# Encoder layer with an expert-choice MoE: the final norm moved beside the last expert, and the order of the last prompt tile and of expert 0 changed

## Chip, cores and metric

One core of a Trainium2 chip. The time is device microseconds of one execution; the kernel is one launch. The engines are named as in the profile: PE (TensorE matmul), PEld (its weight loads), ACT (ScalarE), DVE (VectorE), POOL (GpSimd), SP (SyncE, which issues most DMAs).

## The reference

Two request groups, 256 prompt tokens and 1024 sample tokens with model width 1024, pass one encoder layer with the same weights: adaLN modulation, two attention branches, an output projection, then a mixture of experts in which each expert chooses its tokens, and a final RMSNorm.

```python
h2 = rms_norm(x, norm2_g) * (1 + sc2) + sh2
x = x + gt2 * expert_choice_moe(h2, w_router, w_e_gate, w_e_up, w_e_down)   # per group
y = rms_norm(x)                                                              # gain norm_f_g

def expert_choice_moe(h, ...):      # t: (n, d)
    aff = softmax(t @ w_router)     # 16 experts
    g, idx = top_k(aff.T, 2 * n // 16)        # 32 prompt rows, 128 sample rows per expert
    xe = t[idx]
    hid = silu(xe @ w_gate) * (xe @ w_up)     # width 2048
    out = zeros.at[idx].add((hid @ w_down) * g)
```

All arithmetic is float32. The kernel builds each float32 product from three bf16 products.

## The kernel before

**Precision.** Each matrix is split in a high bf16 half (a cast) and a low bf16 half (the value less the high half). `split_product` multiplies high by high, high by low and low by high (lines 1620 to 1622).

**Experts.** For an expert, `gate_up(f)` makes 128 of the 2048 hidden columns for 160 rows (128 sample, 32 prompt), f from 0 to 15. ScalarE takes the SiLU (L1142), VectorE multiplies by the up part (L1552, `product`), GpSimd splits the hidden values in halves (L816, L819). `down` multiplies by the down weights (L1621, and L1986 for the prompt rows). The down products of expert e run inside expert e+1; those of the last expert stand alone at the end. VectorE evacuates them in `evacuate_down` (L1531, L1533) with the router's weight and the gate.

**Weights.** An expert has 12 chunks of 2 MB, four each of gate, up and down. A chunk is loaded by SP into one of three float32 stages, by kind. ScalarE casts its two halves (L895), VectorE subtracts (L1515, `split_low`, which raises `lo_done`), and the bf16 halves stand in one of six slots. SP waits for `lo_done` of both halves before it loads the stage anew (L628, L634). Expert 0's first eight halves (0 to 7) are prepared beforehand, their low halves by GpSimd (`low_first`, L727). In expert 0 ScalarE does, for each f, the cast of half f+8 and then the SiLU of f, while VectorE does the subtraction of half f+8 and then product f. Halves 8 to 15 are the rest of expert 0 (8, 9 gate; 10, 11 up; 12, 13 gate; 14, 15 up); after them come halves of expert 1 and the down chunk of expert 0.

**The order of steps.** `plan_steps` writes a list that all engines walk. For a token tile `O` is the output product, `XO` the residual add and norm, `X2` the turn to columns with modulation, `RT` the router product and its exponential, `AT` the turn of the scores. `OL` is the output product of the last prompt tile in four parts (two for each column half), `XS` turns and modulates the gathered sample rows of expert 0, `FH` and `FL` are high and low halves of expert 0's first weights, `KM`/`K`/`IS`/`I` are the top-k and its indices. Engines wait for each other by semaphores alone.

**Gather and scatter.** An expert's rows are gathered from memory by an indirect DMA of GpSimd (L716), turned on TensorE, modulated on VectorE and split on GpSimd. Results are added to the accumulator in memory by two indirect DMAs (L828 sample, L830 prompt rows in quarters of 256 columns); L836 follows when they have landed. The prompt rows of expert 0 have their own path: turned at L1954, modulated at L1519, split on GpSimd at L850 and L853, behind `low_first(5)` and `low_first(6)`.

**End.** SP waits for the last expert's down products and its scatter, loads the gain and all ten tiles of 128 rows (L692, L694); ScalarE squares and sums (L1165), VectorE scales to a mean (L1580), ScalarE takes the root (L1167), VectorE the reciprocal (L1582) and the product (L1583), and SP stores (L697).

Of the kernel before, what the change touches and what calls it, by code (L numbers as in the profile page):

```python
# [19 lines left out]
ALU = mybir.AluOpType  # L20
# [80 lines left out]
def plan_steps(items):  # L101
# [98 lines left out]
    for m in range(KD):  # L200
# [5 lines left out]
        for _ in range((0, 0, 2, 3, 3, 3, 3, 2)[m]):  # L206
# [4 lines left out]
          ("FL", 3), ("OL", 0), ("OL", 1), ("X2", ns), ("OL", 2), ("RT", ns), ("OL", 3), ("AT", ns), ("XO", ns + 1),  # L211
          ("X2", ns + 1), ("XS",), ("RT", ns + 1), ("AT", ns + 1)]
# [19 lines left out]
def encoder(nc, x_p, x_s, c_p, c_s, w_ada, b_ada, n1g, w_in, qg, kg, sink, w_ba, w_bb, w_out, n2g, w_router,  # L232
# [25 lines left out]
    with ExitStack() as ctx:  # L258
# [91 lines left out]
        nfb = at(2 * NT * D, D)  # L350
        fin = at(0, NT, D)
        finy = at(10240, NT, D)
# [91 lines left out]
        f_ss, f_v, f_sq, y_ready, y_out = sem("f_ss"), sem("f_v"), sem("f_sq"), sem("y_ready"), sem("y_out")  # L444

# [104 lines left out]
        def _(sp):  # L550
# [138 lines left out]
            sp.wait_ge(dn_done, 8 * NE)  # L689
            sp.wait_ge(sca[0], 16 * NE)  # L690
            sp.wait_ge(sca[1], 16 * NE)
            sp.dma_start(nfb, nfg.partition_broadcast(P)).then_inc(nf_in, 16)  # L692
            for t in range(NT):
                sp.dma_start(fin[:, t], token_rows(acc_d, t)).then_inc(f_in[t], 16)  # L694
            for t in range(NT):
                sp.wait_ge(y_ready, t + 1)
                sp.dma_start(token_rows(y_d, t), finy[:, t]).then_inc(y_out, 16)  # L697
# [4 lines left out]
        def _(gp):  # L702
# [26 lines left out]
            for s in steps:  # L729
# [56 lines left out]
                if k == "XO" and s[1] == NT - 1:  # L786
# [7 lines left out]
                    gp.tensor_tensor(dst[:, 1], xs32, dst[:, 0], ALU.subtract)  # L794
# [44 lines left out]
            for b in range(2):  # L839
# [17 lines left out]
            def expert_pool(e, par, first=False, last=False):  # L857

                h0 = 11 * e + 4
# [21 lines left out]
            scatter(NE - 1, 4 * NE - 2)  # L881
# [3 lines left out]
        def _(ac):  # L885
# [277 lines left out]
            for t in range(NT):  # L1163
                ac.wait_ge(f_in[t], 16)
                ac.activation(finy[:, t], fin[:, t], ACT.Square, accum_out=rs[:, t % 2, 4:5]).then_inc(f_ss, 1)  # L1165
                ac.wait_ge(f_v, t + 1)
                ac.activation(rs[:, t % 2, 6:7], rs[:, t % 2, 5:6], ACT.Sqrt).then_inc(f_sq, 1)  # L1167


        @block.vector  # L1170
        def _(ve):
# [27 lines left out]
            def modulate(s, dst, A, sh, g, halves=(0, 1)):  # L1199

                for half in halves:
# [5 lines left out]
                    ins.then_inc(free, 1)  # L1207

# [42 lines left out]
            for s in steps:  # L1251
# [177 lines left out]
                if k == "M2":  # L1429
# [4 lines left out]
                    if b:  # L1434
                        ins.then_inc(mm_ready, 1)
                if k == "XO":
# [6 lines left out]
                    ve.wait_ge(xo_in[t % 2], 16 * (t // 2 + 1))  # L1443
                    if t >= 2:
                        ve.wait_ge(x1_out[t % 2], 16 * (t // 2))
                    if t < NT - 1:
# [4 lines left out]
                        norm_in(NT + t)  # L1451
                    else:
                        for h in range(2):
                            z = slice(512 * h, 512 * h + 512)
                            ve.wait_ge(*((half_done, 1), (out_done, NT))[h])
                            ve.tensor_tensor(x1[:, t % 2, z], ps[:, 2 * (t % 2) + h], gt1b[g][:, z], ALU.mult).then_inc(last_mul, 1)
                            ve.wait_ge(last_mul, h + 1)
                            ve.tensor_tensor(x1[:, t % 2, z], x1[:, t % 2, z], xo[:, t % 2, z], ALU.add).then_inc(x1_half, 1)
                        ve.wait_ge(ssq, 2 * NT + 1)
                        link(ve.tensor_tensor(rs[:, t % 2, 0:1], rs[:, t % 2, 0:1], rs[:, t % 2, 4:5], ALU.add))  # L1460
                        norm_in(NT + t)
# [54 lines left out]

            ve.wait_ge(xe_done, 3)
# [3 lines left out]
            ins.then_inc(xe_mod, 3)  # L1521

# [13 lines left out]
            def expert_vec(e, par, kind):  # L1536
# [518 lines left out]
```

## Time and profile before

| what | value |
|---|---|
| median of 3 runs (range) | 2432.73 us (2430.87 to 2434.41) |
| the profiled execution, its time | 2433.03 us |
| its span, first to last instruction | 2431.2 us |
| mean granted TensorE clock | 0.98 |
| PE busy | 2317.6 us, 95% |
| DVE busy | 1629.0 us, 67% |
| ACT busy | 1216.5 us, 50% |
| POOL busy | 1109.1 us, 46% |
| DMA moved | 523.29 MB, mean 215 GB/s |

Busy time is the time in which an engine had an instruction in work; the span leaves out what lies around it, so the profiled execution's own time is 1.8 us longer. Row times are microseconds from the span's start. The experts run from 1073 us to 2392 us.

### The profile page before, as it was taken

The numbers are of one execution on the slowest core, as the hardware profiler recorded it, in microseconds if no ns is written. First come the engines' busy times: TensorE is split into PE (matmuls) and PEld (weight loads), VectorE is DVE, ScalarE is ACT, GpSimd is POOL, SyncE is SP. The second block draws the span as 40 slices with busy tenths as digits, with TensorE's granted clock in tenths as the row PEclk, the third lists the DMA queues.
The fourth block names the chain that finished last, engine by engine and source line by source line (L and its number), as shares of the span: only waits on it lengthen the run. The fifth ranks groups of instructions, "written<-read, shape, count | busy, mean of one in ns | idle before, by whom it ended". The sixth has DMA issues, their size and how long they took to land.

```text
span 2431.2 us, 54392 instructions
## 1 busy us (share of the span) xinstructions
PE 2317.6 (95%) x23617; PEld 1688.2 (69%) x23724; DVE 1629.0 (67%) x2034; ACT 1216.5 (50%) x1536; POOL 1109.1 (46%) x706
## 2 busy tenths in 40 slices
PE   8998999999999999959999999999999999999993
PEld 3554676665444457748888888888888888888871
DVE  4765665464222455848887888788779887887872
ACT  4224555475111235345666555655565565556552
POOL 0000111122322214466566776677667766776641
PEclk9998999999999999979999999999999999999997
DMA  9102101502212345378999999989998999999965
GB/s 332 36 18 87 36 1 36 174 1 62 52 53 52 104 157 156 106 254 281 323 331 318 317 334 326 319 317 332 333 320 319 321 342 313 317 327 337 315 246 203
DMA packets 252293, 523.29 MB, mean 215 GB/s; under 512 B 8491, under 2 KB 57756, under 8 KB 251932
## 3 DMA queue, kind: packets, MB, share of 16 engines
q1 hardware_dynamic: 241500, 488.38, 57.6%
q0 software_dynamic: 10560, 31.46, 4.6%
q8 instruction: 188, 3.08, 0.5%
q14 instruction: 45, 0.37, 0.0%
HBM read 491.50 MB, written 28.31 MB: 214 GB/s over the span
## 4 chain that ended last, share of the span: by engine, by line
PE 88%; DVE 4%; DMA 3%; ACT 2%; issue 2%; POOL 1%; SPq 1%; DVEq 0%; ACTq 0%; POOLq 0%
PE ps L1621 23%; PE ps L1622 22%; PE ps L1620 22%; PE ps L1792 4%; PE ps L1780 4%; PE ps L1986 4%; PE ps L1761 3%; DMA arena<-w_e_up 1%; PE ps L1771 1%; PE ps L1681 1%; DMA arena<-w_in 1%; PE ps L1633 1%; PE ps L1719 1%; PE ps L1801 1%; PE ps L1945 1%
## 5 line engine op out<-in xcount | busy, mean ns | idle before, releaser
L1621 PE MATMUL ps<-arena 128*128 128x160 bf16 (+2 forms) x5554 | 1387.9, 268 | 9.7 <-issue 3.0
L1622 PE MATMUL ps<-arena 128*128 128x160 bf16 (+2 forms) x5556 | 1388.4, 268 | 0.3
L1620 PE MATMUL ps<-arena 128*128 128x160 bf16 (+2 forms) x5463 | 1354.3, 266 | 10.7 <-POOL arena L853 6.4
L1515 DVE TENSOR_TENSOR arena<-arena 128x2048 bf16<-128x2048 f32 x376 | 918.8, 2447 | 204.7 <-ACT arena L895 204.2
L895 ACT ACTIVATE arena<-arena 128x2048 bf16<-128x2048 f32 x384 | 726.8, 1904 | 249.1 <-PE ps L1622 179.7
L1620 PEld LDWEIGHTS ps<-arena 128*128 128x128 bf16 x5560 | 545.3, 98 | 166.5 <-issue 14.9
L1622 PEld LDWEIGHTS ps<-arena 128*128 128x128 bf16 x5560 | 545.4, 98 | 153.1 <-issue 0.8
L1621 PEld LDWEIGHTS ps<-arena 128*128 128x128 bf16 x5560 | 545.4, 98 | 140.8 <-issue 1.1
L819 POOL TENSOR_TENSOR arena<-arena 128x320 bf16<-128x320 f32 x128 | 273.8, 2139 | 10.0
L816 POOL TENSOR_TENSOR arena<-arena,ones 128x320 bf16<-128x320 f32 x128 | 176.2, 1376 | 173.0 <-DVE arena L1552 172.7
L1142 ACT ACTIVATE arena<-ps 128x160 f32<-128x160 f32 x256 | 77.5, 303 | 295.3 <-PE ps L1622 295.1
L738 POOL TENSOR_TENSOR arena<-ones,rinv 128x512 f32<-128x512 f32 x20 | 20.9, 1043 | 338.4 <-DVE rinv L1390 279.8
L1427 DVE TENSOR_TENSOR arena<-arena,ps 128x512 f32<-128x512 f32 x32 | 20.6, 684 | 177.9 <-ACT arena L1080 177.9
L1016 ACT ACTIVATE arena<-ps 128x512 f32<-128x512 f32 (+2 forms) x160 | 74.5, 494 | 100.3 <-PE ps L1780 95.7
L805 POOL TENSOR_TENSOR arena<-arena,ones 128x480 bf16<-128x480 f32 (+1 forms) x45 | 103.0, 2288 | 39.6 <-DVE arena L1507 39.5
L1780 PEld LDWEIGHTS ps<-ident,arena 128*128 128x128 f32 x752 | 82.1, 143 | 54.9 <-issue 43.6
L1080 ACT ACTIVATE arena<-ps 128x512 f32<-128x512 f32 x32 | 17.4, 595 | 203.1 <-PE ps L1622 203.1
L755 POOL TENSOR_TENSOR arena<-arena 128x512 f32<-128x512 f32 (+1 forms) x24 | 26.1, 1088 | 193.5 <-DVE arena L1427 171.4
L1780 PE MATMUL ps<-ident,arena 128*128 128x128 f32 x752 | 110.6, 285 | 3.1 <-ACT arena L1005 1.4
L1552 DVE TENSOR_TENSOR arena<-arena,ps 128x160 f32<-128x160 f32 x256 | 79.8, 312 | 41.7 <-POOL arena L819 41.5
L1792 PE MATMUL ps<-arena 128*64 128x128 f32 x1504 | 101.6, 281 | 5.9 <-ACT arena L1016 5.0
L1363 DVE TENSOR_REDUCE nm<-ps 128x1 f32<-128x1024 f32 (+1 forms) x80 | 81.2, 1059 | 38.4 <-PE ps L1761 32.1
(229 smaller groups left out, 2246.8 us busy)
## 6 DMA issues: line engine op xcount, KB each, us to landing
arena<-w_e_gate SPq DMA_DIRECT2D x64, 2048.0 KB, 9.1
arena<-w_e_up SPq DMA_DIRECT2D x64, 2048.0 KB, 9.5
arena<-w_e_down SPq DMA_DIRECT2D x64, 2048.0 KB, 9.0
arena<-w_ada SPq DMA_DIRECT2D x12, 2048.0 KB, 9.0
arena<-w_in SPq DMA_DIRECT2D x30, 512.0 KB, 5.3
arena<-x_sample SPq DMA_DIRECT2D x16, 512.0 KB, 3.6
arena<-w_in SPq DMA_DIRECT2D x3, 2048.0 KB, 16.6
arena<-w_out SPq DMA_DIRECT2D x2, 2048.0 KB, 9.1
```

Source lines behind the costliest of these rows:

```text
L805: gp.tensor_tensor(xeT[par][:, 0, d0:d1], src, ones[:, 0:d1 - d0].unsqueeze(2).to_broadcast([P, d1 - d0, SLOTS]), ALU.mult).then_inc(high, 1)
L816: gp.tensor_tensor(hidT[par][:, 0, f:f + 2], src, ones[:, 0:2].unsqueeze(2).to_broadcast([P, 2, SLOTS]), ALU.mult).then_inc(high, 1)
L819: gp.tensor_tensor(hidT[par][:, 1, f:f + 2], src, hidT[par][:, 0, f:f + 2], ALU.subtract).then_inc(hid_done, 1)
L895: ac.activation(split_half(slot, a)[0], stage_half(kind, a), ACT.Copy).then_inc(hi_done, 1)
L1363: ve.tensor_reduce(nm[:, i % 4, hh:hh + 1], src, AX.X, ALU.max, negate=True).then_inc(nm_ready, 1)
L1515: ve.tensor_tensor(lo, stage_half(kind, a), hi, ALU.subtract).then_inc(lo_done, 1)
L1620: pe.matmul(out, w_hi, x_hi, start=start, stop=False)
L1621: pe.matmul(out, w_hi, x_lo, start=False, stop=False)
L1622: return pe.matmul(out, w_lo, x_hi, start=False, stop=stop)
L1780: ins = pe.transpose(b[:, q * P:(q + 1) * P], probs(i, hh)[:, (a + q) * P:(a + q + 1) * P], ident[:])
L1792: ins = pe.matmul(ps[hh * 64:hh * 64 + 64, 4, j * P:(j + 1) * P], V[:, br, kt, hh * 64:hh * 64 + 64], PTs[br][:, i % 2, hh, n, :], start=( ...
L1986: ins = pe.matmul(ps[32 * g:32 * g + 32, banks[2], 0:256], x, wv[n][:, kf, 256 * g:256 * g + 256], start=q + kf == 0 and x is x_hi and n = ...
```

## The change

In words:

1. The final norm's loads wait for the scatter of expert 14, not of expert 15. The norm is written in place (`fin`), the squares go to a scratch area, and the mean of tile t+1 is computed before the reciprocal of tile t. The last expert's results are not scattered with an add: GpSimd gathers the accumulator's rows that they belong to, VectorE adds, ScalarE squares, a one-column matmul sums the four quarters of the prompt rows, and the finished rows are written over the output by two indirect DMAs after all plain stores have landed. VectorE takes up the last evacuation after six tiles of the norm.
2. The first column half of the last prompt tile (`XH`) goes ahead of the router step of the tile before; `XO` of the last tile does the second half alone and goes ahead of `AT` of the tile before. `XS` goes ahead of `X2` of the first prompt tile.
3. The prompt rows of expert 0 are split by VectorE; GpSimd's `low_first(6)` waits until this is done.
4. In expert 0 VectorE does product f and then the subtraction of half f+7 (`splits(f - 1)`).

```diff
-          ("FL", 3), ("OL", 0), ("OL", 1), ("X2", ns), ("OL", 2), ("RT", ns), ("OL", 3), ("AT", ns), ("XO", ns + 1),
-          ("X2", ns + 1), ("XS",), ("RT", ns + 1), ("AT", ns + 1)]
+          ("FL", 3), ("OL", 0), ("OL", 1), ("XS",), ("X2", ns), ("XH",), ("OL", 2), ("RT", ns), ("OL", 3), ("XO", ns + 1),
+          ("AT", ns), ("X2", ns + 1), ("RT", ns + 1), ("AT", ns + 1)]
...
-            sp.wait_ge(dn_done, 8 * NE)
-            sp.wait_ge(sca[0], 16 * NE)
-            sp.wait_ge(sca[1], 16 * NE)
+
+            sp.wait_ge(lo_done, 24 * NE)
+            sp.wait_ge(xe_done, 3 * NE)
             sp.dma_start(nfb, nfg.partition_broadcast(P)).then_inc(nf_in, 16)
+            for g in range(4):
+                sp.dma_start(nfP[32 * g:32 * g + 32], nfg[256 * g:256 * g + 256].partition_broadcast(32)).then_inc(nf_in, 16)
+            sp.wait_ge(sca[0], 16 * (NE - 1))
+            sp.wait_ge(sca[1], 16 * (NE - 1))
             for t in range(NT):
                 sp.dma_start(fin[:, t], token_rows(acc_d, t)).then_inc(f_in[t], 16)
             for t in range(NT):
                 sp.wait_ge(y_ready, t + 1)
...
             low_first(5)
+            gp.wait_ge(xe_ready, 3)
             low_first(6)
-            gp.wait_ge(xe_mod, 3)
-            dst = xeT[0][:, :, :, CAP_S:SLOTS]
-            gp.tensor_tensor(dst[:, 0], xp32, ones[:, 0:KD].unsqueeze(2).to_broadcast([P, KD, CAP_P]), ALU.mult)\
-                .then_inc(high, 2)
-            gp.wait_ge(high, 3)
-            gp.tensor_tensor(dst[:, 1], xp32, dst[:, 0], ALU.subtract).then_inc(xe_ready, 3)
             low_first(7)
...
-            scatter(NE - 1, 4 * NE - 2)
+
+            def by_quarter(x):
+                return x.rearrange("t (g n) -> (t g) n", g=4)
+
+            gp.tensor_copy(sidx[0][:], idx4[:, NE - 1:NE]).then_inc(cidx, 1)
+            gp.tensor_copy(sidx[1][:], idx[1][:, NE - 1:NE]).then_inc(cidx, 1)
+            gp.wait_ge(cidx, 4 * NE)
+            gp.wait_ge(xe_done, 3 * NE)
+            turn(1)
+            gp.indirect_dma_start(out=rowS, out_offset=None, in_=acc_d[1],
+                                  in_offset=bass.IndirectOffsetOnAxis(ap=sidx[1][:, 0:1], axis=0)).then_inc(gat[1], 16)
+            gp.indirect_dma_start(out=rowP, out_offset=None, in_=by_quarter(acc_d[0]),
+                                  in_offset=bass.IndirectOffsetOnAxis(ap=sidx[0][:, 0:1], axis=0)).then_inc(gat[0], 16)
+            gp.wait_ge(y_out, 16 * NT)
+            gp.wait_ge(row_ready[1], 1)
+            turn(0)
+            gp.indirect_dma_start(out=y_d[1], out_offset=bass.IndirectOffsetOnAxis(ap=sidx[1][:, 0:1], axis=0),
+                                  in_=yeS, in_offset=None).then_inc(row_out[1], 16)
+            gp.wait_ge(row_ready[0], 1)
+            gp.indirect_dma_start(out=by_quarter(y_d[0]), out_offset=bass.IndirectOffsetOnAxis(ap=sidx[0][:, 0:1], axis=0),
+                                  in_=yeP[:], in_offset=None).then_inc(row_out[0], 16)
+            for b in range(2):
+                gp.wait_ge(row_out[b], 16)
...
+            ac.wait_ge(lo_done, 24 * NE)
+            squares(0)
+            for t in range(1, NT):
+                squares(t)
+                root(t - 1)
+            for h in range(2):
+                ac.wait_ge(row_add, h + 1)
+                ac.activation(junk[:, 2, 512 * h:512 * h + 512], yeS[:, 512 * h:512 * h + 512], ACT.Square,
+                              accum_out=rs[:, h, 0:1]).then_inc(f_ss, 1)
+            ac.wait_ge(row_add, 3)
+            ac.activation(junk[:, 3, 0:256], yeP[:], ACT.Square, accum_out=rs[:, 1, 2:3]).then_inc(f_ss, 1)
+            root(NT - 1)
...
+            def last_half(h):
+
+                t = NT - 1
+                z = slice(512 * h, 512 * h + 512)
+                ve.wait_ge(*((half_done, 1), (out_done, NT))[h])
+                ve.tensor_tensor(x1[:, t % 2, z], ps[:, 2 * (t % 2) + h], gt1b[0][:, z], ALU.mult).then_inc(last_mul, 1)
+                ve.wait_ge(last_mul, h + 1)
+                ve.tensor_tensor(x1[:, t % 2, z], x1[:, t % 2, z], xo[:, t % 2, z], ALU.add).then_inc(x1_half, 1)
...
+            ve.wait_ge(out_done, NT)
             ve.wait_ge(xe_done, 3)
             for d in range(KD):
                 ins = ve.tensor_scalar(xp32[:, d], ps[:, 6, d * CAP_P:(d + 1) * CAP_P], A2[:, d, 0:1], modT[:, 24 + d, 0:1],
                                        ALU.mult, ALU.add)
             ins.then_inc(xe_mod, 3)
+            ve.wait_ge(xe_mod, 3)
+            dst = xeT[0][:, :, :, CAP_S:SLOTS]
+            link(ve.tensor_copy(dst[:, 0], xp32))
+            ve.tensor_tensor(dst[:, 1], xp32, dst[:, 0], ALU.subtract).then_inc(xe_ready, 3)
...
                 if kind == "first":
                     for f in range(KF):
-                        if f < KF - 1:
-                            splits(f)
                         product(f)
+                        if f:
+                            splits(f - 1)
                         if f in (7, 9, 11):
                             modulate_rows(3, (f - 7) // 2, 1)
                     splits(KF - 1)
...
+            mean(0)
+            ve.wait_ge(nf_in, 16 * 5)
+            for t in range(NT):
+                if t == 6:
+                    evacuate_down(NE - 1)
+                    ve.wait_ge(gat[1], 16 * NE + 16)
+                    for h in range(2):
+                        x = yeS[:, 512 * h:512 * h + 512]
+                        ve.wait_ge(ye_done, 3 * NE - 1 + h)
+                        ve.tensor_tensor(x, x, rowS[:, 512 * h:512 * h + 512], ALU.add).then_inc(row_add, 1)
+                    ve.wait_ge(gat[0], 16 * NE + 16)
+                    ve.wait_ge(ye_done, 3 * NE + 1)
+                    ve.tensor_tensor(yeP[:], yeP[:], rowP, ALU.add).then_inc(row_add, 1)
+                if t + 1 < NT:
+                    mean(t + 1)
                 ve.wait_ge(f_sq, t + 1)
                 link(ve.reciprocal(rs[:, t % 2, 7:8], rs[:, t % 2, 6:7]))
-                ve.scalar_tensor_tensor(out=finy[:, t], in0=fin[:, t], scalar=rs[:, t % 2, 7:8], in1=nfb,
+                ve.scalar_tensor_tensor(out=fin[:, t], in0=fin[:, t], scalar=rs[:, t % 2, 7:8], in1=nfb,
                                         op0=ALU.mult, op1=ALU.mult).then_inc(y_ready, 1)
+                if t == NT - 2:
+                    ve.wait_ge(f_ss, NT + 2)
+                    link(ve.tensor_tensor(rs[:, 0, 1:2], rs[:, 0, 0:1], rs[:, 1, 0:1], ALU.add))
+                    ve.tensor_scalar(rs[:, 0, 2:3], rs[:, 0, 1:2], 1.0 / D, EPS, ALU.mult, ALU.add).then_inc(f_v, 1)
+                    ve.wait_ge(row_sum, 1)
+                    ve.tensor_scalar(rst[:, 0, 1:2], ps[:, 0, 0:1], 1.0 / D, EPS, ALU.mult, ALU.add).then_inc(f_v, 1)
+            ve.wait_ge(f_sq, NT + 1)
+            link(ve.reciprocal(rs[:, 1, 1:2], rs[:, 0, 3:4]))
+            ve.scalar_tensor_tensor(out=yeS, in0=yeS, scalar=rs[:, 1, 1:2], in1=nfb, op0=ALU.mult, op1=ALU.mult)\
+                .then_inc(row_ready[1], 1)
+            ve.wait_ge(f_sq, NT + 2)
+            link(ve.reciprocal(rst[:, 0, 3:4], rst[:, 0, 2:3]))
+            ve.scalar_tensor_tensor(out=yeP[:], in0=yeP[:], scalar=rst[:, 0, 3:4], in1=nfP, op0=ALU.mult, op1=ALU.mult)\
+                .then_inc(row_ready[0], 1)
...
+            pe.wait_ge(fold_ready, 1)
+            pe.wait_ge(f_ss, NT + 3)
+            pe.wait_ge(prod_done, 16 * NE)
+            pe.matmul(ps[:, 0, 0:1], fold.rearrange("p a b -> p (a b)"), rs[:, 1, 2:3], start=True, stop=True).then_inc(row_sum, 1)
```

## Rows read from the trace of the kernel before

**Rows 1.** Windows, expert loop: us, PE to POOL busy (count), PEclk, DMA share, GB/s.
```profile
1160.00:1240.00 80.00, 79.69 (x1042) 66.37 (x1044) 65.35 (x59) 46.99 (x40) 41.10 (x24) 1.00 0.91 312
```

**Rows 2.** Timelines, last prompt tile, DVE and ACT: start us, us, instruction, [idle before].
```profile
1042.14 0.69 DVE L1456 TENSOR_TENSOR arena<-ps,arena 128x512 f32<-128x512 f32 x1
...
1049.49 2.90 ACT L1071 ACTIVATE arena<-ps,modT,A 128x128 f32<-128x128 f32 x8
...
1051.52 0.17 DVE L1469 TENSOR_REDUCE rst<-ps 128x1 f32<-128x16 f32 x1 [3.04 <-PE ps L1925]
```

**Rows 3.** Timelines, split of expert 0's prompt rows, DVE and POOL.
```profile
1066.99 1.84 DVE L1519 TENSOR_SCALAR arena<-ps,A,modT 128x32 f32<-128x32 f32 x8 [4.97 <-PE ps L1954]
...
1063.82 8.09 POOL L727 TENSOR_TENSOR arena<-arena 128x2048 bf16<-128x2048 f32 x2
1071.85 0.63 POOL L850 TENSOR_TENSOR arena<-arena,ones 128x256 bf16<-128x256 f32 x1
```

**Rows 4.** Timeline of SP's queue, loads of expert 0's weights.
```profile
1067.93 0.37 SPq L628 DMA_DIRECT2D arena<-w_e_gate  x1
1077.34 0.37 SPq L628 DMA_DIRECT2D arena<-w_e_up  x1
1083.78 0.37 SPq L628 DMA_DIRECT2D arena<-w_e_gate  x1
```

**Rows 5.** Timelines, expert 0, ACT (cast, SiLU) and DVE (product, subtraction).
```profile
1087.53 1.91 ACT L895 ACTIVATE arena<-arena 128x2048 bf16<-128x2048 f32 x1 [5.62 <-DMA arena<-w_e_up]
1089.35 0.29 ACT L1142 ACTIVATE arena<-ps 128x160 f32<-128x160 f32 x1
...
1091.68 0.31 DVE L1552 TENSOR_TENSOR arena<-arena,ps 128x160 f32<-128x160 f32 x1
1091.91 2.29 DVE L1515 TENSOR_TENSOR arena<-arena 128x2048 bf16<-128x2048 f32 x1
...
1120.50 3.15 DVE L1515 TENSOR_TENSOR arena<-arena 128x2048 bf16<-128x2048 f32 x1 [1.24 <-ACT arena L895]
```

**Rows 6.** Timeline of POOL, the last two scatters.
```profile
2377.30 0.19 POOL L836 TENSOR_TENSOR spare<-ones 128x1 f32<-128x1 f32 x1 [3.47 <-DMA acc_prompt<-yeP,sidx_p]
...
2393.85 0.19 POOL L798 TENSOR_TENSOR spare<-ones 128x1 f32<-128x1 f32 x1 [16.12 <-DVE yeP L1533]
...
2401.40 0.19 POOL L836 TENSOR_TENSOR spare<-ones 128x1 f32<-128x1 f32 x1 [3.49 <-DMA acc_prompt<-yeP,sidx_p]
```

**Rows 7.** Timeline of DVE, last evacuation and final norm.
```profile
2391.90 1.41 DVE L1531 SCALAR_TENSOR_TENSOR arena<-ps,gv_s,arena 128x512 f32<-128x512 f32 x2 [22.33 <-PE ps L1986]
...
2409.98 1.28 DVE L1583 SCALAR_TENSOR_TENSOR arena<-arena,rs 128x1024 f32<-128x1024 f32 x1
2411.18 0.15 DVE L1580 TENSOR_SCALAR rs<-rs 128x1 f32<-128x1 f32 x1
...
2426.33 1.28 DVE L1583 SCALAR_TENSOR_TENSOR arena<-arena,rs 128x1024 f32<-128x1024 f32 x1
```

**Rows 8.** Timeline of ACT, first tile of the final norm.
```profile
2407.09 1.06 ACT L1165 ACTIVATE arena<-arena 128x1024 f32<-128x1024 f32 x1 [41.55 <-DMA arena<-acc_prompt]
...
2408.25 1.28 ACT L1167 ACT_TABLE_LOAD   x1
```

**Rows 9.** The page's DMA issues: count, KB each, us to landing.
```profile
arena<-x_sample SPq DMA_DIRECT2D x16, 512.0 KB, 3.6
```

**Rows 10.** DMA issues 1020 to 1045: KB each, us from issue to landing.
```profile
arena<-w_e_gate SPq DMA_DIRECT2D x1, 2048.0 KB, 8.1
```

**Rows 11.** Expert 1's start (timelines), then PE by windows: us, busy, PEclk, DMA.
```profile
1136.09 0.32 DVE L1552 TENSOR_TENSOR arena<-arena,ps 128x160 f32<-128x160 f32 x1 [0.20 <-ACT arena L1142]
...
1136.55 0.23 PE L1620 MATMUL ps<-arena 128*128 128x160 bf16 x1 [0.84 <-DVE arena L1552]
...
1122.00:1124.00 2.00, 0.06 (x1) 1.00 1.05 402
1124.00:1126.00 2.00, 2.00 (x17) 0.52 0.50 179
```

More of the change, by code:

```diff
@@ L857, in expert_pool @@
             def expert_pool(e, par, first=False, last=False):
-                h0 = 11 * e + 4
+                h0 = 11 * e + 3
                 if not last:
@@ L1162, in _, with squares, root @@
             expert_act(NE - 1, "last")
-            for t in range(NT):
+            def squares(t):
                 ac.wait_ge(f_in[t], 16)
-                ac.activation(finy[:, t], fin[:, t], ACT.Square, accum_out=rs[:, t % 2, 4:5]).then_inc(f_ss, 1)
+                ac.activation(junk[:, t % 2], fin[:, t], ACT.Square, accum_out=rs[:, t % 2, 4:5]).then_inc(f_ss, 1)
+            def root(t):
                 ac.wait_ge(f_v, t + 1)
                 ac.activation(rs[:, t % 2, 6:7], rs[:, t % 2, 5:6], ACT.Sqrt).then_inc(f_sq, 1)
+            ac.wait_ge(lo_done, 24 * NE)
[10 more added lines that the diff above has]
+            root(NT - 1)
+            ac.wait_ge(f_v, NT + 1)
+            ac.activation(rs[:, 0, 3:4], rs[:, 0, 2:3], ACT.Sqrt).then_inc(f_sq, 1)
+            ac.wait_ge(f_v, NT + 2)
+            ac.activation(rst[:, 0, 2:3], rst[:, 0, 1:2], ACT.Sqrt).then_inc(f_sq, 1)
         @block.vector
@@ L1435, in _ @@
                         ins.then_inc(mm_ready, 1)
+                if k == "XH":
+                    ve.wait_ge(xo_in[(NT - 1) % 2], 16 * (NT // 2))
+                    ve.wait_ge(x1_out[(NT - 1) % 2], 16 * ((NT - 1) // 2))
+                    last_half(0)
                 if k == "XO":
@@ L1450, in _ @@
                         ve.tensor_tensor(x1[:, t % 2], x1[:, t % 2], xo[:, t % 2], ALU.add).then_inc(x1_ready, 1)
-                        norm_in(NT + t)
                     else:
[L1453 to L1458, printed above, removed]
+                        last_half(1)
                         ve.wait_ge(ssq, 2 * NT + 1)
                         link(ve.tensor_tensor(rs[:, t % 2, 0:1], rs[:, t % 2, 0:1], rs[:, t % 2, 4:5], ALU.add))
-                        norm_in(NT + t)
+                    norm_in(NT + t)
                     ve.tensor_scalar(xn2[:, t % 2], x1[:, t % 2], rs[:, t % 2, 3:4], None, ALU.mult).then_inc(xn2_ready, 1)
@@ L1575, in _ @@
             expert_vec(NE - 1, 1, "last")
-            evacuate_down(NE - 1)
-            ve.wait_ge(nf_in, 16)
-            for t in range(NT):
+            ve.wait_ge(xe_done, 3 * NE)
+            link(ve.tensor_tensor(fold[:, 0], ident[:, 0:32], ident[:, 32:64], ALU.add))
+            for g in (2, 3):
+                link(ve.tensor_tensor(fold[:, 0], fold[:, 0], ident[:, 32 * g:32 * g + 32], ALU.add))
+            ve.tensor_copy(fold[:, 1:4], fold[:, 0:1].to_broadcast([P, 3, 32])).then_inc(fold_ready, 1)
@@ L1579, in _, with mean @@
+            def mean(t):
                 ve.wait_ge(f_ss, t + 1)
                 ve.tensor_scalar(rs[:, t % 2, 5:6], rs[:, t % 2, 4:5], 1.0 / D, EPS, ALU.mult, ALU.add).then_inc(f_v, 1)
+            mean(0)
[13 more added lines that the diff above has]
+                    mean(t + 1)
@@ L1999, in expert_tensor @@
             def expert_tensor(e, par, kind):
+                if kind == "first":
+                    pe.wait_ge(high, 2)
                 pe.wait_ge(xe_ready, 3 * e + 3)
```

18 lines of the change are left out of this document (10 added, 8 removed).

## The prediction, made before the change was timed

> **What bounds the kernel now.** I read the windows view first: in an expert of the steady loop TensorE is busy 79.69 of 80 us at the full granted clock [rows 1]. Nothing in that loop is edited, and whatever moves the start of expert 1 moves the end by the same amount, because there is no idle TensorE time behind it to absorb a delay or to give back a gain. So the change can act in two places only: the passage from the last prompt tile to expert 1, and the tail behind the last down product. The chain of waits and the timelines by engine then show what is late in each.
>
> In the passage the order is: last prompt tile, router, top-k, gather, modulation, GpSimd's split of the prompt rows, first gate/up product [rows 2, 3]. From there TensorE is not the bound but the refill of the two weight stages: a 2 MB load, two ScalarE casts, two VectorE subtractions, and only then the next load into that stage [rows 4, 5]. In the tail TensorE has finished when the last evacuation starts at 2391.90, and the span ends at 2431.2: 39.3 us in which a scatter, a reload of all rows and ten tiles of norm run one behind the other [rows 6 to 8].
>
> **The tail, step by step.** SP no longer waits for the last expert's scatter but for the one before, which is over when GpSimd's L836 runs at 2377.30 [rows 6]. Issued at 2377.4, the first 512 KB tile lands after 3.6 us, the median of such loads [rows 9], at 2381.0. ScalarE squares two tiles (1.15 us each with the accumulator read, from 2407.09 to 2408.25), loads the Sqrt table (1.28) and takes the root (0.2) [rows 8]: 2384.8. Reciprocal and product take 0.2 and 1.28 [rows 7], so tile 0 is ready at 2386.3. Before, one tile took 1.81 us, because VectorE and ScalarE waited for each other; now the mean of the next tile is computed ahead and VectorE's own work is the bound: 1.20 from the product's start to the mean's start, 0.08 and 0.20 for the two small ones [rows 7], 1.5 us a tile. Tiles 0 to 5 are ready at 2393.8. That is 1.9 us after the last down product, so the evacuation now waits for VectorE and not for TensorE.
>
> Evacuation takes 1.8 us [rows 7]; three adds of the gathered rows, two of 512 elements at 0.61 to 0.69 [rows 2] and one of 256 at an estimated 0.4, 1.7 us: 2397.3. Tiles 6, 7, 8: 2401.8. One add and two means for the special rows, 0.5 us as ScalarE's squares and TensorE's 1-column product lie beside tiles 7 and 8; tile 9: 2403.9. Its store lands 3.6 us later, as before (product ends 2427.61, span ends 2431.2) [rows 7]: 2407.5. VectorE's two products on the special rows (1.7 us) lie inside that landing. GpSimd then turns over and issues two indirect stores; the same pair took from 2393.85 to 2401.40, 7.55 us, before [rows 6], where it added to memory. I take the same for the plain form, and 1.5 less as the other bound. End: 2415.1, against 2431.2, so **-16.1 us**. The new read of the last expert's rows by GpSimd starts at 2378 and is needed at 2395; the new broadcasts of the gain are issued at 2368. Both have 10 us of cover. The tile loads are issued in one stretch on SP and no store waits behind them before 2386. Bounds: -17.6 (faster store) and -12.5 (loads that land at the 5.3 us seen in the old reload, and 2 us of waiting between ScalarE and VectorE).
>
> **The passage, up to expert 0.** The first half of the last tile (two operations of 0.69) and the copy of the router's transposed scores leave VectorE's path ahead of the second half; the second half, which started at 1042.14 [rows 2], can start when TensorE's last output product of the tile ends, 1040.2: -1.9. ScalarE's eight modulations of the sample rows (2.90 from 1049.49) stood in front of the exponential, whose operand was ready at 1051.7 [rows 2]: -0.5. They go to a place where ScalarE idled six microseconds for the router, and TensorE's eight transposes go into its idle stretch 1030.3 to 1032.26, behind a gather that landed in 4.4 us at 1030.6. Top-k, indices and gather thus come 2.4 us earlier. Bounds: 1.0 (the gather lands late and holds TensorE's queue, behind it the tile's own transposes) and 2.4.
>
> The prompt rows' split: VectorE's modulation ended at 1068.83 [rows 3], now 1066.4. Two operations of 256 elements, 0.3 to 0.45 each from half the 0.69 row [rows 2], give 1067.2. GpSimd did it at 1071.85 to 1073.3, behind two low halves [rows 3]. So TensorE starts expert 0 6 us earlier. This is worth nothing by itself: the first SiLU stands on ScalarE behind the cast of a half whose load lands later. What counts is when loads start. GpSimd's low half 5 ends 2.4 us earlier, so the gate load goes at 1065.5 and not 1067.93. Low halves 6 and 7 now wait for 1067.2 and take 8.1 us [rows 3]: the up load goes at 1075.3 and not 1077.34 [rows 4], **-2.0**.
>
> **VectorE's order in expert 0.** Before, it did split(f), product(f). Now it does product(f), split(f-1). ScalarE's order is unchanged: cast(f), then SiLU(f). Halves 9 and 10 lie in different stages. The subtraction of half 9 frees the gate stage. Before, it ran ahead of product 1, and the next gate load was issued at 1083.78 while the up load of 1077.34 was in flight [rows 4]. Now it runs behind product 2, which needs SiLU 2, which stands behind the cast of half 10, the first of the **up** load. So each load is issued only after the other stage's load has landed: the overlap of two loads is gone.
>
> One link of this new chain: cast started to SiLU started 1.82 us; to the product 0.33; product start to subtraction start 0.23; subtraction 2.3 [rows 5]: 4.7 us, then a lone load. Lone loads of 2 MB took 8.1, three of them [rows 10]; add 0.1 to the cast. A link is 12.9 us, for one load. Before, two loads shared one turn of some 16.9: the up load of 1077.34 was cast from 1087.53 and its stage was free again at 1094.2 [rows 4, 5].
>
> The first up load took 10.19 to its cast at 1087.53 [rows 4, 5], with the next gate load and expert 1's rows beside it; now only the rows are beside it, and I take 9.5, between 8.2 and 10.2: cast at 1084.8. Five links follow (gate, up, gate, up of the next chunks, and the load that SiLU 14 waits for): 1084.8 + 64.5 = 1149.3. Product 14 at 1151.5, one subtraction, product 15 at 1154.0, first product of expert 1 0.46 later [rows 11]: 1154.5, where it was 1136.55. **+18.0 us** including the -2.0. TensorE idles some 3.5 us ahead of it. After 2 us of idling at 1122 to 1124 it came back at 0.52 of its clock for over 3 us [rows 11], which costs half of that: **+1.6**. Together +19.6. Bounds: 16.6 (no clock loss, first load 8.2) and 24 (rival B).
>
> A page speaks against the size of this term. The Trainium skill, "DMA: Bandwidth & Descriptors", section "Anatomy of one DMA", gives a load a fixed 2.0 us and 436 GB/s beyond that, thus an estimated 6.8 us for 2 MB; the front would then be 7 us less, and the time 2429.6. The trace disagrees (8.1 us), and the sum goes by the trace.
>
> **Sum.** 2431.2 + 19.6 - 16.1 = 2434.7. The profiled execution took 2433.03, 1.8 us more than its span: 2436.5. The median of the runs is 0.3 lower than that execution: 2436.2, in round numbers **2436.4**, +0.15%. A measurement of this kernel can tell about 0.2% (4.9 us) from no change, so the forecast is no change that can be told, leaning to slower. Its own range is 2430 to 2441.
>
> **Rivals.** A: the refill keeps its overlap (I misread which subtraction frees which stage, or the weight casts run ahead of the SiLU). Then the front gives its 2.0 us and the tail 16.1: 2414.6. For it speaks that TensorE starts earlier and that VectorE has idle time in this stretch; against it, that ScalarE's rows show cast, SiLU, cast, SiLU in strict turn [rows 5]. Chance 0.14.
>
> B: slower than forecast. The subtraction sits in each link, and beside GpSimd's splits it took 3.15 us and not 2.29 [rows 5]. The new order puts it right behind a product, which is what releases GpSimd. If all five links and the two at the end pay 0.86, the front is 6 us longer: 2442.4. It decides when GpSimd's pair and the freeing subtraction fall together; against it, GpSimd is released by the odd products and the freeing subtraction follows an even one. Chance 0.18. The Trainium skill, "SBUF — State Buffer", section "Who interferes with whom", says a VectorE operation with two SBUF inputs and a GpSimd read exclude each other; the 3.15 us row agrees.
>
> C: a lone load lands earlier than rows 10 say. From the tile load (3.6 us for 0.52 MB [rows 9]) and 1.57 MB more at 402 GB/s [rows 11] a load would take 7.5 us, and five links are 3.3 us shorter: 2433.1, no change. Three lone loads at 8.1 speak against it. Chance 0.06. The DMA page named above goes the same way, and further.
>
> The forecast keeps 0.62. Faster by over 0.2% (below 2427.8): A and 0.06 of the forecast, 0.20. Slower (above 2437.6): B and 0.19 of the forecast, 0.37. Within: C and 0.37 of the forecast, 0.43. The range leaves out A and the top of B: 2427 to 2444.
>
> **What would show it.** Expert 0: weight loads on SP one at a time, 12 to 13 us apart, from the third on; expert 1's first product near 1154; TensorE idle in four to five gaps of about 6 us between 1090 and 1154. The first product of expert 0 at 1067. In the tail, loads from 2397 on (all times of the loop shift by some 19.6), six norm tiles before the last evacuation, the span ending 23 to 25 us behind the last down product where it was 39.3. Wrong would be: two weight loads in flight through expert 0 (A), subtractions over 3 us on the chain (B), or SiLU waiting for TensorE and not for casts.

## The result, and the profile after

The changed kernel takes 2439.26 us (median of 11 runs, 2434.29 to 2442.06), the kernel before 2428.72 (11 runs, 2423.05 to 2434.41): a ratio of 1.0044, 95% interval 1.0034 to 1.0055. It is slower, by 10.5 us and by more than the 0.2% that can be told. The forecast of 2436.4 was 2.9 us below the time and its range (2427 to 2444) holds it. But it stood on a profiled execution of before of 2433.03, which lies 4.3 above the later median of before; as a difference the forecast was +3.7 us, and the difference measured is +10.5. That the time itself came so near is luck in part: with the median of before that all eleven runs give, the same sum ends at 2432.4.

The profiled execution of after took 2437.55 us, its span is 2435.8. The two traces can't be subtracted time by time. Tile 8's norm product stands far ahead of any edited step, and it starts at 1030.66 before and at 1024.09 after: 6.6 us that come from unchanged code. The two executions as a whole differ by about as much in chance: the one of before took 4.3 us more than its kernel's median, the one of after 1.7 less. So I count from that product in the front, and from the last down product in the tail.

**Expert 0.** SP's queue of loads after, to be set against [rows 4] (start us, us, instruction):

```profile
1058.79 0.37 SPq L631 DMA_DIRECT2D arena<-w_e_gate  x1
1068.88 0.37 SPq L631 DMA_DIRECT2D arena<-w_e_up  x1
1084.56 0.37 SPq L631 DMA_DIRECT2D arena<-w_e_gate  x1
1098.06 0.37 SPq L631 DMA_DIRECT2D arena<-w_e_up  x1
1111.62 0.37 SPq L631 DMA_DIRECT2D arena<-w_e_gate  x1
1124.42 0.37 SPq L631 DMA_DIRECT2D arena<-w_e_up  x1
1137.32 0.39 SPq L631 DMA_DIRECT2D arena<-w_e_gate  x1
```

Before, the gate load at 1083.78 went out 6.4 us behind the up load of 1077.34. Now it goes 15.7 us behind it, and the next ones 13.5, 13.6, 12.8 and 12.9 us apart. One link in the chain of waits after (start us, us, what):

```profile
1084.56 8.79 DMA arena<-w_e_gate
1093.52 1.68 issue
1095.19 0.29 ACT arena L1166
1095.55 0.20 issue
1095.75 2.29 DVE arena L1566
1098.06 8.85 DMA arena<-w_e_up
```

A load lands, the cast of its half runs (the 1.68 us of "issue"), SiLU follows behind it, a product (the 0.20), the subtraction, and only then the other stage's load starts. Two windows, one in expert 0 and one in the steady loop (us, PE, PEld, DVE, ACT, POOL busy and count, PEclk, DMA share, GB/s):

```profile
1090.00:1122.00 32.00, 19.63 (x217) 18.61 (x214) 11.66 (x15) 10.45 (x11) 9.06 (x6) 0.82 0.43 155
1160.00:1240.00 80.00, 80.00 (x1046) 66.38 (x1044) 64.18 (x58) 47.68 (x39) 46.73 (x28) 1.00 0.88 317
```

In the first TensorE is busy 61% of the time, no engine is near full and the DMA engines work 43% of it: a chain, not an engine, sets the time. In the second nothing can be given back, as [rows 1] said.

Expert 1's first product, timelines of DVE and PE:

```profile
1150.15 0.31 DVE L1608 TENSOR_TENSOR arena<-arena,ps 128x160 f32<-128x160 f32 x1
```

```profile
1150.61 0.23 PE L1713 MATMUL ps<-arena 128*128 128x160 bf16 x1 [4.19 <-DVE arena L1608]
```

Against [rows 11] (1136.55) it is 14.1 us later, and counted from tile 8's norm product 20.6. From there to the last down product it takes 1256.9 us where it took 1255.3: +1.6.

**The passage.** The prompt rows' split on DVE, and what follows on POOL, against [rows 3]:

```profile
1057.98 1.84 DVE L1571 TENSOR_SCALAR arena<-ps,A,modT 128x32 f32<-128x32 f32 x8 [5.11 <-PE ps L2047]
1059.86 0.29 DVE L1576 CAST arena<-arena 128x256 bf16<-128x256 f32 x1
1060.26 0.42 DVE L1577 TENSOR_TENSOR arena<-arena 128x256 bf16<-128x256 f32 x1
```

```profile
1060.76 8.10 POOL L734 TENSOR_TENSOR arena<-arena 128x2048 bf16<-128x2048 f32 x2 [1.99 <-DVE arena L1577]
```

Counted from the norm product the gate load is issued 2.6 us earlier and the up load 1.9.

**The tail.** DVE after: first tile, sixth tile, last evacuation, tile 9, the two products on the special rows:

```profile
2402.09 1.29 DVE L1661 SCALAR_TENSOR_TENSOR arena<-arena,rs 128x1024 f32<-128x1024 f32 x1
...
2409.36 1.28 DVE L1661 SCALAR_TENSOR_TENSOR arena<-arena,rs 128x1024 f32<-128x1024 f32 x1
2410.56 1.41 DVE L1587 SCALAR_TENSOR_TENSOR arena<-ps,gv_s,arena 128x512 f32<-128x512 f32 x2
...
2418.69 1.28 DVE L1661 SCALAR_TENSOR_TENSOR arena<-arena,rs 128x1024 f32<-128x1024 f32 x1
...
2420.08 1.28 DVE L1671 SCALAR_TENSOR_TENSOR arena<-arena,rs 128x1024 f32<-128x1024 f32 x1
...
2421.47 0.48 DVE L1675 SCALAR_TENSOR_TENSOR yeP<-yeP,rst,arena 128x256 f32<-128x256 f32 x1
```

The last down product ends at 2407.5 and the span at 2435.8: 28.3 us behind it, where it was 39.3 [rows 7]. So the two traces differ by -6.6 (unchanged code) + 20.6 + 1.6 - 11.0 = +4.6 us, and without the first term by +11.2, beside the +10.5 measured.

POOL's last instructions after, and then, of SP's waits by releaser (us in total, times, longest), the one at the end, before and after:

```profile
2424.01 0.19 POOL L805 TENSOR_TENSOR spare<-ones 128x1 f32<-128x1 f32 x1 [27.70 <-DMA y_sample<-arena]
2424.35 1.00 POOL L899 DMA_INDIRECT y_sample<-arena,sidx_s  x1
2425.66 0.98 POOL L902 DMA_INDIRECT y_prompt<-yeP,sidx_p  x1 [0.30 <-issue]
```

```profile
SPq L258 <- PEq L258: 0.2, 1, 0.2
```

```profile
SPq L258 <- PEq L258: 11.6, 1, 11.6
```

L258 is no line of work but the `with` line around the whole program; I read waits at it as the meeting of all engines at the end. Before, SP stood there for 0.2 us once its last tile store had landed, and the program was over. Now it stands there for 11.6 us, and POOL's last store was issued 10 us before the end.

### The profile page after: what moved, and what is told of

It reads as the page before. It is cut to its first block, busy times and chain, and to the rows that moved or that the text cites. A ratio compares the mean times of both kernels' runs of the same rounds, so it can differ in the third digit from the quotient of the medians.

```text
span 2435.8 us, 54538 instructions
## 1 busy us (share of the span) xinstructions
PE 2330.7 (96%) x23726; PEld 1696.0 (70%) x23726; DVE 1632.4 (67%) x2050; ACT 1218.0 (50%) x1544; POOL 1115.7 (46%) x706
## 4 chain that ended last, share of the span: by engine, by line
PE 88%; DMA 4%; DVE 3%; ACT 2%; issue 2%; POOL 1%; SPq 1%; ACTq 0%; DVEq 0%; POOLq 0%
PE ps L1713 23%; PE ps L1715 22%; PE ps L1714 22%; PE ps L1885 4%; PE ps L1873 4%; PE ps L2079 3%; PE ps L1854 3%; DMA arena<-w_e_up 1%; DMA arena<-w_e_gate 1%; PE ps L1864 1%; PE ps L1774 1%; DMA arena<-w_in 1%; PE ps L1726 1%; PE ps L1894 1%; PE ps L2038 1%
## 5 line engine op out<-in xcount | busy, mean ns | idle before, releaser
L1713 PE MATMUL ps<-arena 128*128 128x160 bf16 (+2 forms) x5560 | 1395.9, 269 | 27.3 <-DVE arena L1608 22.0
L1714 PE MATMUL ps<-arena 128*128 128x160 bf16 (+2 forms) x5560 | 1396.0, 269 | 0.0
L1715 PE MATMUL ps<-arena 128*128 128x160 bf16 (+2 forms) x5560 | 1395.9, 269 | 0.0
L826 POOL TENSOR_TENSOR arena<-arena 128x320 bf16<-128x320 f32 x128 | 279.8, 2186 | 10.0
L823 POOL TENSOR_TENSOR arena<-arena,ones 128x320 bf16<-128x320 f32 x128 | 187.9, 1468 | 188.8 <-DVE arena L1608 188.5
L745 POOL TENSOR_TENSOR arena<-ones,rinv 128x512 f32<-128x512 f32 x20 | 20.9, 1043 | 335.6 <-DVE rinv L1444 277.0
L1481 DVE TENSOR_TENSOR arena<-arena,ps 128x512 f32<-128x512 f32 x32 | 20.6, 684 | 176.2 <-ACT arena L1104 176.2
```

The costliest lines, as they stand in the source:

```text
L823: gp.tensor_tensor(hidT[par][:, 0, f:f + 2], src, ones[:, 0:2].unsqueeze(2).to_broadcast([P, 2, SLOTS]), ALU.mult).then_inc(high, 1)
L826: gp.tensor_tensor(hidT[par][:, 1, f:f + 2], src, hidT[par][:, 0, f:f + 2], ALU.subtract).then_inc(hid_done, 1)
L1713: pe.matmul(out, w_hi, x_hi, start=start, stop=False)
L1714: pe.matmul(out, w_hi, x_lo, start=False, stop=False)
L1715: return pe.matmul(out, w_lo, x_hi, start=False, stop=stop)
```

## The experiments

Each is compared with runs of the kernel before that were taken beside it: 2429.54 us (e1 to e4), 2427.39 (e5 to e8), 2428.35 (e9, e10). e2 and e4 are edits of the kernel before, e3 is the kernel before with the new tail, and all others are edits of the changed kernel.

**e1, e2, e3, e4: the change in its three parts.** e1 is all but VectorE's new order, e2 is that order alone in the kernel before:

```diff
                 if kind == "first":
                     for f in range(KF):
+                        if f < KF - 1:
+                            splits(f)
                         product(f)
-                        if f:
-                            splits(f - 1)
```

> The changed kernel with one edit undone: in expert 0 VectorE again does the subtraction of half f+8 and then product f; the passage and the tail stay as changed. Theory 1 (the reorder takes away the overlap of two weight loads, some +22 us): the loads on SP's queue are again issued while the other stage's is in flight, two in some 16 us, expert 1's first product comes 22 us earlier than in the changed kernel counted from the last prompt tile's norm, and the kernel is 13 to 16 us faster than before (ratio 0.9935 to 0.9947). Rival (the loss in expert 0 comes from the passage: VectorE's split of the prompt rows and GpSimd waiting for it): no gain over the changed kernel, ratio 1.003 to 1.005.

> The kernel before with one edit alone: product f, then the subtraction of half f+7, in expert 0. Theory 1: loads one at a time 12.8 to 13.6 us apart, expert 1's first product 21 to 24 us later than before (the up load starts at its old time), ratio 1.0085 to 1.010. Rival (the edits only hurt together): within 0.2% of before.

e3 is the new tail alone, e4 is all edits of the passage alone (`XH`, `XS`, `last_half`, the split of the prompt rows):

```diff
e3: ...
    +            sp.wait_ge(sca[0], 16 * (NE - 1))
    ...
e4: ...
    +            dst = xeT[0][:, :, :, CAP_S:SLOTS]
    +            link(ve.tensor_copy(dst[:, 0], xp32))
    +            ve.tensor_tensor(dst[:, 1], xp32, dst[:, 0], ALU.subtract).then_inc(xe_ready, 3)
    ...
```

> The kernel before with the new tail alone (norm beside the last down products, last expert's rows gathered and stored at the end). Theory: the span ends 28.3 us behind the last down product and not 39.3, so 11 us faster, ratio 0.9950 to 0.9960. My forecast's step had 16 us (ratio 0.9934). Rival (the tail's traffic disturbs the last products or the gain is taken back by the end of the program): under 5 us.

> The kernel before with the passage alone: the last prompt tile's first half and the sample rows' turning moved ahead, the prompt rows split on VectorE, GpSimd's low half 6 waiting for it; neither the reorder nor the new tail. Theory: TensorE starts expert 0 six us earlier, but the up load starts only 2 us earlier, and the refill of the stages is what sets expert 1's start: 2 us faster, ratio 0.999. Rival (the start of TensorE counts in full): 6 us faster, ratio 0.9975.

The difference is the ratio less 1, times 2429.54:

| | us (range) | ratio to before (interval) | difference |
|---|---|---|---|
| e1, without the new order | 2415.99 (2414.17 to 2417.19) | 0.9945 (0.9931 to 0.9958) | -13.4 |
| e2, the new order alone | 2450.63 (2448.16 to 2457.70) | 1.0086 (1.0072 to 1.0099) | +20.9 |
| e3, the tail alone | 2418.82 (2416.07 to 2420.71) | 0.9958 (0.9944 to 0.9971) | -10.2 |
| e4, the passage alone | 2427.50 (2424.74 to 2430.88) | 0.9996 (0.9987 to 1.0005) | -1.0 |

The three parts sum to +20.9 - 10.2 - 1.0 = +9.7, and the whole, by its ratio, +10.7: they add up. The new order costs twice what the tail gives. In e2's trace the loads are issued one at a time, 12.5 to 14.9 us apart, and expert 1's first product comes 24.3 us later than before; the expectation had 12.8 to 13.6 and 21 to 24. That execution (2457.70) is the slowest of its five, so the +20.9 of the times is the better figure. In e3's trace the tail behind the last down product took 29.2 us and not the 28.3 expected, 10.2 less than before. SP's loads in e1 show the overlap back, in steps of 10.0, 7.0, 10.9 and 6.0 us:

```profile
1060.64 0.37 SPq L631 DMA_DIRECT2D arena<-w_e_gate  x1
1070.60 0.37 SPq L631 DMA_DIRECT2D arena<-w_e_up  x1
1077.60 0.37 SPq L631 DMA_DIRECT2D arena<-w_e_gate  x1
1088.48 0.37 SPq L631 DMA_DIRECT2D arena<-w_e_up  x1
1094.46 0.37 SPq L631 DMA_DIRECT2D arena<-w_e_gate  x1
```

and expert 1's first product, counted from tile 8's norm product, 23.0 us earlier than in the changed kernel (103.5 against 126.5 us), near the difference of the two times (23.3 as they stand, 24.1 by the ratios). In e4 the same distance is 103.4 us against 105.9 before: in the traces the passage is worth 2.5 us. The times alone can't tell that from nothing (-3.2 to +1.2).

**e5 and e7: which of the two orders closes the chain.** The chain needs two things together: VectorE's subtraction one product late, and ScalarE's SiLU behind the cast of a later load. e5 takes away the second and e7 the first:

```diff
-                        if f < KF - 1:
-                            splits(f)
                         silu(f)
-                    splits(KF - 1)
+                        splits(f)
```

```diff
                         product(f)
-                        if f:
-                            splits(f - 1)
+                        if f < KF - 1:
+                            splits(f)
```

> The changed kernel, VectorE's new order kept, but ScalarE in expert 0 does the SiLU of f and then the cast of half f+8. Theory 1 (the freeing subtraction of half 9 stands behind product 2, which stands behind SiLU 2, which stands behind the cast of the other stage's load): with the SiLU ahead of the cast that chain is cut, loads overlap again, and the time is that of the kernel without the reorder, ratio 0.993 to 0.996. Rival (a subtraction behind a product is slow by itself, as it meets GpSimd's split): still slower than before, ratio 1.003 or more.

> The changed kernel with VectorE's order in expert 0 as product f, then the subtraction of half f+8 (and not f+7). The product still goes first. Theory 1: the subtraction of half 9 follows product 1, whose SiLU stands behind the cast of half 9 itself and not of the other stage's half 10; loads overlap, ratio 0.993 to 0.996. Rival (the product going first is what costs): 1.003 or more.

e5 took 2418.89 us (2412.21 to 2421.37), ratio 0.9962 (0.9948 to 0.9976); e7 2418.95 (2416.72 to 2422.75), 0.9967 (0.9954 to 0.9980). By these ratios e5 is 9.2 and e7 8.0 us faster than before, where the changed kernel is 10.7 slower and e1 13.4 faster: each undoes 19 to 20 of 24 us. What is left of the difference to e1 is 4 to 5 us, and the intervals touch. The traces show some 3 us of it. Expert 1 starts 1.5 (e5) and 0.6 us (e7) later than in e1, counted from tile 8's norm product, and from there to the last down product they take 1256.6 and 1256.7 us where e1 takes 1255.3: the granted clock of expert 1's first 5 us is 0.72 and 0.73 there and 1.00 in e1. In e7 the tail is 0.9 us longer as well. e3, with the order of before, has the slow start too (0.66, 1257.0 us), so it is not the order's own, and what decides on it stays open. In e5 the gate load goes 7.9 us behind the up load. SP's loads in e7:

```profile
1069.60 0.37 SPq L631 DMA_DIRECT2D arena<-w_e_up  x1
1077.65 0.37 SPq L631 DMA_DIRECT2D arena<-w_e_gate  x1
1087.78 0.37 SPq L631 DMA_DIRECT2D arena<-w_e_up  x1
```

The gate load goes 8.05 us behind the up load, where it was 15.7. In e7 the product still stands ahead of the subtraction, so "product first" does little harm by itself; the lag of one does. This shows the mechanism from both sides: product f waits for SiLU f, SiLU f for the cast of half f+8, and with a lag of one the subtraction that frees a stage stands behind a product whose SiLU waits for the other stage's load.

**e6, e8, e9, e10: the 7.5 us at the end.** In e6 SP waits for the landing of the last two stores and GpSimd does not; e8 lets GpSimd wait and puts an operation on one column behind its waits, as a mark in the trace.

```diff
e6, GpSimd:  ...
             -            for b in range(2):
             -                gp.wait_ge(row_out[b], 16)
    SP:      +            for b in range(2):
             +                sp.wait_ge(row_out[b], 16)
e8, GpSimd:  +            gp.tensor_tensor(endp[:], ones[:, 0:1], ones[:, 1:2], ALU.add)
```

> The changed kernel, but SP and not GpSimd waits for the landing of the last two indirect stores. In the trace of the changed kernel they land at 2428.3 and the span ends at 2435.8, 7.5 us with nothing in it. Theory 2a (GpSimd needs some 7 us to finish its program after the waits): with the waits on SP, GpSimd's finishing starts some 1.7 us earlier, 1.5 to 2 us faster than the changed kernel. Theory 2b (the finishing begins with the issue of the last store whatever waits): no change. Theory 2c (GpSimd's wait for its own stores is late by 7 us): 7 us faster.

> The changed kernel with one GpSimd operation on one column behind its last waits. Its start shows when the waits were over. Theory 2a and 2b: 2.6 to 3 us after the issue of the last store, with some 7 us of nothing behind it. Theory 2c: some 7 us later, right ahead of the end.

e6: 2436.11 us (2432.34 to 2442.14), ratio to before 1.0035 (1.0020 to 1.0051). e8, a single run: 2437.81. The mark in e8 says when the stores have landed, and thus that landing is not what fills the end:

```profile
2428.48 0.19 POOL L907 TENSOR_TENSOR endp<-ones 128x1 f32<-128x1 f32 x1 [1.69 <-DMA y_prompt<-yeP,sidx_p]
```

The span of e8 ends at 2436.0, 7.3 us behind the mark. e9 is e1 with e6's edit. e10 is e1 with the two last stores left out (the rows of the last expert keep the values of the tiles' stores), GpSimd ending with the mark:

```diff
e10: ...
     -            turn(0)
     -            gp.indirect_dma_start(out=y_d[1], ...).then_inc(row_out[1], 16)
                  gp.wait_ge(row_ready[0], 1)
     -            gp.indirect_dma_start(out=by_quarter(y_d[0]), ...).then_inc(row_out[0], 16)
     -            for b in range(2):
     -                gp.wait_ge(row_out[b], 16)
     +            gp.tensor_tensor(endp[:], ones[:, 0:1], ones[:, 1:2], ALU.add)
```

> The changed kernel with the old VectorE order in expert 0 (2416.0 us, turn of GpSimd at 2401.25, span 2413.0, 11.75 us behind the turn) and with SP instead of GpSimd waiting for the landing of the last two indirect stores. Theory 1 (GpSimd's end of program takes some 7.5 us from its last instruction, and starts 1.7 to 2 us earlier when it does not wait): turn to end 9.9 to 10.1 us as in e6, time about 2414.2. Theory 2 (the end of the program waits for the stores anyway, and e6's 1.8 us were chance): turn to end 11.7 us, time 2416.

> The changed kernel with the old VectorE order in expert 0, leaving out the two last indirect stores (the last expert's rows are then the ones before it in the output); GpSimd waits for VectorE's two products on these rows and ends with an operation on one column. Theory 1a (the end of the program costs GpSimd some 7.5 us behind its last instruction, of whatever kind): its last operation falls at some 2401.4 and the span ends at 2408.9 (time 2411.5). Theory 1b (the 7.5 us belong to indirect transfers just issued): the span ends when the store of tile 9 has landed, about 2401 to 2402, at most 1 us behind GpSimd's last operation (time 2404).

e9: 2415.11 us (2411.66 to 2419.48), ratio 0.9948 (0.9929 to 0.9966). e10: 2411.16 (two runs). The last POOL instruction of e9, then of e10:

```profile
2401.55 0.98 POOL L904 DMA_INDIRECT y_prompt<-yeP,sidx_p  x1 [0.30 <-issue]
```

```profile
2399.96 0.19 POOL L900 TENSOR_TENSOR endp<-ones 128x1 f32<-128x1 f32 x1 [28.05 <-DMA y_sample<-arena]
```

| | POOL's last instruction ends | what it is | span ends | distance |
|---|---|---|---|---|
| e6 | 2427.45 | indirect store | 2434.8 | 7.35 |
| e8 | 2428.67 | mark behind the stores' landing | 2436.0 | 7.3 |
| e9 | 2402.53 | indirect store | 2409.9 | 7.4 |
| e10 | 2400.15 | mark, no store at all | 2407.3 | 7.15 |

Whatever comes last on GpSimd, store or mark, the program is over 7.2 to 7.4 us behind it. (In the changed kernel GpSimd still waits for its stores to land behind its last instruction, so the distance from that instruction is 9.2 us there.) Theory 1b (the time belongs to indirect transfers just issued) wanted e10 to end at 2401 to 2402; it ended at 2407.3, near the 2408.9 of theory 1a. Before, POOL was done at 2401.6 [rows 6], and 7.4 us from there is 2409, well inside the norm. So this time was always there and became visible when the change made GpSimd the last engine. Letting SP wait takes the landing out of that path: from GpSimd's turn to the end 10.0 us in e6 and e9, 11.8 in e1, e8 and the changed kernel. In the times this 1.8 us is too small to tell (e6 and the changed kernel, e9 and e1 overlap). What GpSimd does in the 7.3 us no trace shows, and all four kernels use its indirect transfers earlier on, so it isn't shown for a kernel without them. The Trainium skill, "Runtime: NRT & Kernel Launch", section "The ~15µs preamble/postamble breakdown", lists about 5 us of barriers and resets behind a kernel; as the span of before ended 0.2 us after SP's last store had landed, these lie outside the span or are hidden in it, and the page names nothing of GpSimd's.

## Why the prediction was right, and where not

**The chain in expert 0** was forecast as it is: "each load is issued only after the other stage's load has landed", one link 4.7 us plus a lone load. Links took 12.8 to 13.6 us, forecast 12.9. Of the five lone loads four took 8.79, 8.85, 8.10 and 8.03 us and the fifth 8.00, forecast 8.1; the first two make +1.4. The first up load took 11.0 us to its cast and not 9.5, beyond the 10.2 that bounded it. This gives +20.6 for the +18.0 forecast. Its bounds of 16.6 to 24 were for the front as a whole, with the clock; the front gave 22.2, inside them. The clock's +1.6 was met to a tenth, and the rows bear out the reason: expert 1's first 5 us ran at a granted clock of 0.66 behind TensorE's idling (1.00 before, in e1 and in e4), and expert 1 to the last down product took 1256.9 us after and 1255.3 to 1255.4 in those three. But the same 1257.0 us in e3, without the chain, show that this cost doesn't need the new order. GpSimd's splits took 2.70 us where they took 0.72, but the subtractions of the five links stayed at 2.28 to 2.30, and the two at the end took 2.57 and 2.51: rival B (3.15) did not come. Rivals A and C are refuted by the loads above. That the order is the cause is shown by e1, e2, e5 and e7, not only argued.

**The page's rule on the load's length.** A lone 2 MB load took 8.0 to 8.9 us in the traces here. The Trainium skill, "DMA: Bandwidth & Descriptors", section "Anatomy of one DMA", gives the fit from which the prediction worked out an estimated 6.8. The section is on transfers that GpSimd issues, and these loads are issued by SP, so the difference does not speak against it; for SP's loads the measured time is what to go by.

**The passage** gave what was forecast for the loads (-2.6 and -1.9 us; forecast -2.4 and -2.0), and -2.5 us at expert 1 in e4, but that is luck in part. "TensorE starts expert 0 6 us earlier. This is worth nothing by itself" holds: it started 6.0 us earlier. The last tile's router products took 3.60 us at a granted clock of 0.50 (window 1040 to 1044), that is at 1.2 GHz, and 1.96 before. The row of after, and the one of before:

```profile
1040.42 3.60 PE L2018 MATMUL ps<-wr,arena 128*128 128x16 f32 x16 [1.59 <-ACT arena L1133]
```

```profile
1049.53 1.96 PE L1925 MATMUL ps<-wr,arena 128*128 128x16 f32 x16
```

It is 3.59 to 3.60 in every other trace too, also in e2 and e3, whose code up to there is that of the kernel before. So it is no cost of the passage: the profiled execution of before was the exception. In e2 and e3 the up load goes out 48.6 us behind tile 8's norm product, in before 46.7, in after 44.8. Against e2 and e3 the passage brings the gate load 4.5 and the up load 3.8 us forward, nearly twice the forecast, and expert 1 in e4 3.4 us against e3. Why the clock rose in that one execution stays open.

**The tail** is where the sum failed: -11.0 us and not -16.1, and this is most of the miss of 7 us. The norm itself was right: first square 3.56 us behind the loads' issue, 1.455 us a tile (forecast 1.5), six tiles ahead of the evacuation, tile 9's product over 12.4 us behind the last down product (forecast 12.0). The second tile landed late (1.4 us of idle time on ScalarE), at the time of GpSimd's two gathers, which are not shown to be the reason, and cost some of the 0.4. Tile 9's landing was another 0.4 late. Then the step "GpSimd then turns over and issues two indirect stores; the same pair took 7.55 us [rows 6] ... I take the same for the plain form": the plain stores took 4.3 us from the turn to the mark of e8 and not 7.55, so 3.2 were won there. And the step after it, "End: 2415.1", put the end of the program at the landing of these stores, with nothing behind it: 7.5 us were missing. In sum 0.4 + 0.4 - 3.2 + 7.5 = +5.1. The rows of before showed only that SP's end is followed by 0.2 us; they could not show what GpSimd's is, because it ended 30 us early.

**The sum.** +1.5 from the first load, +1.0 from the links and +5.1 from the tail make 7.6 of difference beyond the +3.5 forecast. The median of before, 4 us lower than that of the three runs shown, brought the time itself back near 2436.4 by luck. (The sum as written gives 2436.2, and "in round numbers 2436.4" rounds it the wrong way.) Slower was thus given too little (0.37), above all because the 7.5 us behind GpSimd's last work were not in the sum: with the tail's 5.1 us the forecast would have been +8.8 us, beyond what can be told.

**The best version** is the changed kernel without VectorE's new order: e1, 2415.99 us, and e9, 2415.11, which can't be told apart. Both are 0.5% faster than before.

## What to carry to other kernels

When work is reordered on an in-order engine, write down for each stage of a double buffer which instruction frees it and everything that this instruction now stands behind, on every engine: here two orders, either of which alone leaves the loads overlapped (e5, e7), together closed a chain that cost some 23 us. When the last work of a program moves to another engine, ask what that engine's own end costs: in the kernel before it was hidden. And time parts of a large change one by one, because a gain of 10 us hid behind a loss of 21.

## What the hardware did that was not expected

- The program ends 7.2 to 7.4 us after GpSimd has nothing left to do or to wait for, be its last instruction an indirect store or an operation on one column (e6, e8, e9, e10, one trace each); in the kernel before it ended 0.2 us after SP's last store had landed.
- Two plain indirect stores took 4.3 us from GpSimd's turn to their landing (e8), the same pair with addition to memory 7.55 (before).
- Profiled executions drift apart in code that all these kernels share: tile 8's norm product starts between 1020.4 (e5) and 1030.7 us (before), so a single pair of traces can't settle a few microseconds unless both are counted from a common instruction near the edit. Even then one execution can be the exception, as before was with its router products (1.96 us against 3.60 in all others).
